# Eight pairs of input-projection tiles a layer as seven block products each, with weight sums by GpSimd

## What is computed

```python
h = _rms_norm(x, mix_norm_g[l])
aq, ak, av, bq, bk, bv, cq, ckv, ckr, gates = _split_cols(h @ w_in[l])   # 512 x6, 384, 256, 32, 3072 columns
oa = differential_attention(aq, ak, av);  ob = dilated_attention(bq, bk, bv);  oc = latent_attention(cq, ckv, ckr)
br = jnp.einsum('bsnc,ncd->bsnd', jnp.stack([oa, ob, oc], axis=2), w_branch[l])
g = jax.nn.sigmoid(gates.reshape(b, s, N_BRANCHES, d))
x = x + jnp.sum(g * br, axis=2) @ w_out[l]
```

## Time and profile before

| | us |
|---|---|
| median of 3 runs | 1645.34 |
| lowest and highest run | 1643.28, 1646.18 |
| span of the profiled execution | 1642.4 |
| PE busy | 1337.7 (81%) |
| DVE busy | 509.3 (31%) |
| ACT busy | 242.0 (15%) |
| POOL busy | 33.6 (2%) |
| mean granted clock of PE | 0.911 |

### The profile page before, as it was taken

How to read it: one execution, slowest core, us unless ns; L and a number is a source line. 1 busy time by engine, 2 the same in 40 slices (tenths; PEclk the granted TensorE clock), 3 DMA queues, 4 the chain that set the end, 5 groups by cost and what they waited for, 6 DMA issues and landing times.

```text
span 1642.4 us, 18217 instructions
## 1 busy us (share of the span) xinstructions
PE 1337.7 (81%) x7594; PEld 793.6 (48%) x7594; DVE 509.3 (31%) x1007; ACT 242.0 (15%) x587; POOL 33.6 (2%) x46
## 2 busy tenths in 40 slices
PE   8999999999666566677699999999996666657655
PEld 7886688755122132233268857886642121312211
DVE  4235464444211211221112462643531211221121
ACT  2214410032010000000021244000410000000002
POOL 2000000001000000000000000000100000000000
PEclk9999999999887888788899999999998787887888
DMA  9933246449999999999995323563699999999996
GB/s 301 328 116 116 78 132 248 175 165 356 412 421 422 420 418 422 421 421 421 419 344 193 122 84 94 192 227 123 250 376 421 421 421 421 419 421 421 421 421 267
DMA packets 143910, 503.87 MB, mean 307 GB/s; under 512 B 9424, under 2 KB 83216, under 8 KB 96720
## 3 DMA queue, kind: packets, MB, share of 16 engines
q1 hardware_dynamic: 140224, 494.41, 77.7%
q0 software_dynamic: 1712, 4.04, 0.8%
q10 hardware_dynamic: 1888, 4.19, 0.7%
HBM read 501.56 MB, written 1.05 MB: 306 GB/s over the span
## 4 chain that ended last, share of the span: by engine, by line
PE 55%; DMA 39%; SPq 2%; DVE 2%; issue 1%; ACT 1%; DVEq 0%; ACTq 0%
DMA ring<-in_w_dram 38%; PE banks L1685 25%; PE banks L1952 6%; PE banks L2020 5%; PE banks L1691 4%; PE banks L2116 3%; SPq L563 2%; PE banks L1849 1%; PE banks L1859 1%; PE banks L1880 1%; PE banks L1901 1%; PE banks L2151 1%; PE banks L2102 1%; PE banks L1743 1%; PE banks L1844 1%
## 5 line engine op out<-in xcount | busy, mean ns | idle before, releaser
L1952 PE MATMUL banks<-ring,v 128*32 128x512 f32 x1888 | 295.8, 759 | 179.4 <-DMA ring<-in_w_dram 168.9
L1685 PE MATMUL banks<-hT,ring 128*128 128x256 f32 x1440 | 317.6, 380 | 0.9 <-ACT kx_wide L836 0.5
L1685 PEld LDWEIGHTS banks<-hT,ring 128*128 128x128 f32 x1440 | 271.9, 190 | 43.3 <-issue 5.3
L1952 PEld LDWEIGHTS banks<-ring,v 128*32 128x32 f32 x1888 | 78.8, 135 | 383.0 <-issue 380.6
L2020 PE MATMUL banks<-ring,probT 128*32 128x512 f32 x960 | 142.6, 716 | 83.6 <-DMA ring<-in_w_dram 76.8
L2020 PEld LDWEIGHTS banks<-ring,probT 128*32 128x32 f32 x960 | 37.3, 129 | 172.7 <-issue 162.6
L1362 DVE COPY q<-banks 128x512 f32<-128x512 f32 x16 | 11.1, 692 | 240.2 <-PE banks L2020 209.2
L1901 PE MATMUL banks<-v,h 128*128 128x128 f32 x512 | 67.0, 293 | 12.1 <-issue 11.7
L1901 PEld LDWEIGHTS banks<-v,h 128*128 128x128 f32 x512 | 63.6, 206 | 26.4 <-issue 26.4
L1358 DVE TENSOR_TENSOR q<-banks,q 128x512 f32<-128x512 f32 x16 | 11.1, 692 | 208.7 <-PE banks L1952 208.7
L1351 DVE TENSOR_SCALAR q<-q 128x512 f32<-128x512 f32 x16 | 6.8, 427 | 162.7 <-ACT q L848 162.7
(11 more groups left out here) (318 smaller groups left out, 1305.3 us busy)
## 6 DMA issues: line engine op xcount, KB each, us to landing
ring<-in_w_dram SPq DMA_DIRECT2D x348, 1024.0 KB, 19.3
ring<-in_w_in_dram SPq DMA_DIRECT2D x52, 1024.0 KB, 9.9
ring<-in_w_branch_dram SPq DMA_DIRECT2D x8, 1024.0 KB, 5.1
ring<-in_w_out_dram SPq DMA_DIRECT2D x8, 1024.0 KB, 5.9
ring<-in_w_dram SPq DMA_DIRECT2D x16, 512.0 KB, 14.4
shared<-in_w_dram SPq DMA_DIRECT2D x6, 1024.0 KB, 5.5
ring<-in_w_branch_dram SPq DMA_DIRECT2D x8, 512.0 KB, 3.4
k<-in_w_dram SPq DMA_DIRECT2D x4, 1024.0 KB, 8.5
```

Source lines behind the costliest of these rows:

```text
L1685: last = nc.tensor.matmul(dst, w[:, k, cols], src[:, k, :], start=k == 0, stop=k == kn - 1)
L1952: last = nc.tensor.matmul(bank[2 + m][e * CAP:(e + 1) * CAP, :], xt[:, k, e * CAP:(e + 1) * CAP], ws[e](r), start=k == 0, stop=k == KD - 1)
```

## The change

Eight pairs of `w_in` tiles a layer are no longer computed as two jobs but as one **double** (`double`): aq, ak, bq, bk (doubles 0 to 3), and gates 4 and 5, 6 and 7, 8 and 9, 10 and 11 (doubles 4 to 7). The product of activations (2 token blocks by 2 K halves) with weights (2 K halves by 2 tiles) is formed from seven block products in place of eight (Winograd's variant of Strassen's scheme).

- **PE**: a block product is 8 matmuls 128x128 by 128x128; a double is 56 of them, in place of 32 with 256 columns. Doubles 0 to 3 now all stand at the start of the layer, before av0; the units of branch A have a job only at every second unit. The gate stage is doubles and branch products in a new order with fixed banks.
- **POOL**: `sum_double` makes the four weight sums of a double, each one tensor_tensor of 128x1024 in SBUF, into two ring slots that SP does not load. Doubles 0 and 1 are summed first in each layer, then the small loads, then doubles 2 to 5, then the router loads and the gain, then doubles 6 and 7.
- **DVE**: `make_halves` forms four sums of blocks of hT (128x512 each) twice a layer; the first time right behind the copies of hT. `join_double` has five instructions of 128x256 for each double. In layer 0 the joins stand behind `set_up_tables`.
- **ACT**: `copy_double` copies five of the block products out of PSUM; for gates `exp_double` follows.
- A layer has 58 turns before the experts in place of 42, and 2 empty turns at its end in place of 6. One preload of an expert tile moves behind the gate doubles. The landing semaphores of a path for overfull experts are halved in number.

The diff, cut to its core:

```diff
+for _at in (OFF_AQ, OFF_AK, OFF_BQ, OFF_BK):
+    add_double(_at, _at + 256)
...
+GATE_DOUBLES = [(4, 5), (6, 7), (8, 9), (10, 11)]
...
+            def sum_double(l, n):
+                at = DOUBLES[n]
+                low, high = (slot_k(at + side, 8, 256) for side in (SIDE_A, SIDE_B))
+                sums = [slot_k(at + SUM_LOW + i // 2, 8, 256)[:, 4 * (i % 2):4 * (i % 2) + 4, :] for i in range(4)]
+                done = (l * ND + n) * 4
+                wait_turn(pool, l, at + SIDE_A)
+                wait_turn(pool, l, at + SIDE_B)
+                pool.wait_ge(slot_free, l * PER_LAYER + (at + SUM_LOW + 1))
+                nc.gpsimd.tensor_tensor(sums[0], low[:, 0:4, :], high[:, 0:4, :], ALU.add).then_inc(sums_made, 1)
+                pool.wait_ge(sums_made, done + 1)
+                nc.gpsimd.tensor_tensor(sums[1], sums[0], high[:, 4:8, :], ALU.add).then_inc(sums_made, 1)
+                pool.wait_ge(slot_free, l * PER_LAYER + (at + SUM_HIGH + 1))
+                nc.gpsimd.tensor_tensor(sums[2], high[:, 0:4, :], high[:, 4:8, :], ALU.add).then_inc(sums_made, 1)
+                pool.wait_ge(sums_made, done + 2)
+                nc.gpsimd.tensor_tensor(sums[3], sums[1], low[:, 4:8, :], ALU.add).then_inc(sums_made, 1)
...
             for l in range(DEPTH):
                 row = one(l)
+                sum_double(l, 0)
+                sum_double(l, 1)
...
+            def make_halves(l, to, late):
...
+                nc.vector.tensor_tensor(to[:, 0], a21, a22, ALU.subtract).then_inc(halves_made, 1)
...
+            def join_double(l, n):
...
+                dve.wait_ge(double_copied, copies + 3)
+                nc.vector.tensor_tensor(high[:, :, 0:P], high[:, :, 0:P], low[:, :, P:], ALU.subtract)\
+                  .then_inc(double_joined, 1)
+                dve.wait_ge(double_made, (l * ND + n) * DOUBLE_MADE + 4)
+                dve.wait_ge(double_joined, done + 1)
+                nc.vector.scalar_tensor_tensor(high[:, :, 0:P], double_bank(n, 2), s, high[:, :, 0:P], ALU.mult, ALU.add)\
+                  .then_inc(double_joined, 1)
...
             for l in range(DEPTH):
                 row = bass.ds(l, 1)
                 copy_hT(l)
+                dve.wait_ge(hT_act, l * COPIES + 2)
+                dve.wait_ge(hT_dve, l * COPIES_DVE + 2)
+                make_halves(l, early_halves, 0)
                 if l == 0:
                     mem_values(0)
                     set_up_tables()
-                for name in ("aq1", "ak1"):
-                    job(l, name)
+                for n in range(NE):
+                    join_double(l, n)
...
+                def others_done(i):
+                    if n % NE >= 2:
+                        if i == 0:
+                            pe.wait_ge(double_copied, (done - 1) * DOUBLE_COPIED)
+                        else:
+                            pe.wait_ge(double_joined, (done - 2) * DOUBLE_JOINED + (5 if i == 1 else 2))
...
+                product(to[0], low[:, 0:4, :], a11, True, ...).then_inc(double_made, 1)
+                others_done(2)
+                pe.wait_ge(halves_made, halves_at + 1)
+                pe.wait_ge(sums_made, done * 4 + 1)
+                product(to[2], sums1[:, 0:4, :], halves[:, 0], True).then_inc(double_made, 1)
...
+                double(l, NE)
+                branches(0)
+                double(l, NE + 1)
+                branches(1)
+                double(l, NE + 2)
+                double(l, NE + 3)
+                branches(2)
+                branches(3)
```

More of the change, by code:

```diff
@@ L121, in add_gate @@
[L121 to L136, removed]
+T_GATE, T_BRANCH = {}, {}
@@ new lines, in gate_col, with add_double, add_branches @@
+def gate_col(g):
+    return OFF_GATE + GATES[g][1] * D + GATES[g][0] * 256
+def add_double(low, high):
+    DOUBLES.append(len(TURNS))
+    TURNS.extend([("in", low), ("in", high), ("sums", 0), ("sums", 1)])
+def add_branches(pair):
+    for n in range(N_BRANCHES):
+        T_BRANCH[pair, n] = len(TURNS) + n // 2
+    TURNS.extend([("branch01", pair), ("branch2", pair)])
+for _at in (OFF_AQ, OFF_AK, OFF_BQ, OFF_BK):
+    add_double(_at, _at + 256)
+T_AV = len(TURNS)
+TURNS += [("in", OFF_AV), ("in", OFF_AV + 256), ("in", OFF_CQ), ("in", OFF_CQ + 256), ("in_last", 3584)]
@@ new lines @@
+T_BV = len(TURNS)
+TURNS += [("in", OFF_BV), ("in", OFF_BV + 256), ("uq", 0), ("uq", 384), ("ukv", 0)]
+T_UQ = T_BV + 2
+for _g in range(EARLY):
+    T_GATE[_g] = len(TURNS)
+    TURNS.append(("in", gate_col(_g)))
+GATE_DOUBLES = [(4, 5), (6, 7), (8, 9), (10, 11)]
+for _pair in range(2):
+    add_double(*[gate_col(_g) for _g in GATE_DOUBLES[_pair]])
+    add_branches(_pair)
+for _pair in range(2, 4):
+    add_double(*[gate_col(_g) for _g in GATE_DOUBLES[_pair]])
+for _pair in range(2, 4):
+    add_branches(_pair)
@@ L357, in bass_hybrid_encoder @@
         main_r, more_r = round_sems("main"), round_sems("more")
[L358 removed]
+        more_landed = [sem(f"more_landed{i}") for i in range(QUAD)]
         more_free = sem("more_free")
@@ L363, in real_turns @@
             return sum(len(CUT_COLS) if CUT <= j < CUT + QUAD else 1 for j in range(upto) if j % RING == slot and
-                       j < PER_LAYER - EMPTY)
+                       j < PER_LAYER - EMPTY and not (j < T_OUT and TURNS[j][0] == "sums"))
         def wait_turn(eng, l, j):
@@ L686, in _ @@
                     load_mcol(l + 1)
+                for n in range(2, NE + 2):
+                    sum_double(l, n)
+                pool.wait_ge(double_joined, (l * ND + NE) * DOUBLE_JOINED)
                 pool.wait_ge(ca_normed, l * 6 + 6)
@@ L702, in _ @@
                 load_gain(ffn_norm_g[row, :])
+                for n in range(NE + 2, ND):
+                    sum_double(l, n)
                 pool.wait_ge(gain_in, l * 16 + 32)
@@ new lines, in _ @@
+                for g in range(3):
+                    sigmoid(g)
+                join_double(l, NE)
+                sigmoid(3)
+                for n in range(3):
+                    mix(0, n)
+                sigmoid(4)
+                sigmoid(5)
+                join_double(l, NE + 1)
+                mix(1, 0)
+                sigmoid(6)
+                mix(1, 1)
+                mix(1, 2)
+                sigmoid(7)
+                join_double(l, NE + 2)
+                sigmoid(8)
@@ L1472, in add_projected @@
+                sigmoid(9)
+                join_double(l, NE + 3)
+                mix(2, 0)
+                sigmoid(10)
+                mix(2, 1)
+                sigmoid(11)
+                mix(2, 2)
+                for n in range(3):
+                    mix(3, n)
                 def add_projected(n, o):
@@ L2058, in _ @@
                 pe.wait_ge(kx_copied, l + 1)
+                for n in range(NE):
+                    double(l, n)
                 job(l, JOB_NAMES[0])
-                pe.wait_ge(vx_copied, l + 1)
-                for name in JOB_NAMES[1:5]:
-                    job(l, name)
                 if l == 0:
```

329 lines of the change are left out of this document (237 added, 92 removed), and 2 rows, old and new, of the table JOBS.

## The result

The changed kernel takes 1676.0 us, median of 4 runs (1672.3 to 1677.2); the kernel before took 1645.8 beside it. The ratio is 1.018, with a 95% interval from 1.0166 to 1.0195: slower, as forecast (1680). The profiled execution has a span of 1670.5 us at a granted clock of 0.902, against 1642.4 and 0.911 before; DVE is busy for 635.3 us and POOL for 189.8, against 509.3 and 33.6.

The account below looks back on a forecast made before the run. PE was taken to bound the mixing part, loads the experts. Layer 0 at +23.0 and layer 1 at +11.4 gave +34.4 on a span of 1642.4: 1676.8, with 2.9 outside it 1680 us; range 1630 to 1695, 8 in 10.

Parts of the forecast that it names:

- Block products: On PE, 0.112 us an instruction, 12.5 us a double against 13.8 for two jobs: 5.3 saved for four doubles.
- POOL's sums: On POOL, a 128x1024 sum takes 2.4 us, four a double 9.6, less than PE's 12.5.
- The late first sums, +2.0: At the very start, turn 1 lands at 27.3 and the first sums come late for PE: 2.0 us added once.
- The tables of layer 0: Layer 0's start: table instructions on DVE take turns with POOL, ending at 78.2; PE waits 23.6 us, plus 2.4 for clock.
- The start of layer 1, +11.1: Seven DVE instructions of the root each wait for a sum: first product 14.0 later, 2.4 for clock, less 5.3.
- Attention, +4.2 a layer: Two sums of double 4 delay DVE at the key rope, +3.2, and double 5's sums add 1.0.
- The 1.0 for double 5: In each layer's attention, double 5's sums fall beside the units of branch C: +1.0 us.
- Gates, -3.9 a layer: Gate stage: 5.9 us saved a layer, less 2.0 of added PE wait.
- The 2.0 that I had added for DVE's lateness: Gate stage: some eight short DVE instructions wait 1 to 2 us each; 2.0 us of PE wait a layer.
- Experts: The experts' part keeps its length, starting earlier or later by whatever the mixing part does.
- Rival A: DVE is hardly held up, by short turns or POOL waiting instead: 1625 us, range 1618 to 1634, chance 20%.
- Rival B: Turns, but cheaper, at 1.28 us a sum: 1645 us, range 1640 to 1662, chance 16%.

Follow-up runs that it names:

- Without sums: The changed kernel with each of GpSimd's 64 additions cut to one element a partition and products reading the low slot instead: 1625.4 us, ratio to before 0.9886.
- with halves: The changed kernel with each sum of 128x1024 made as two additions of 128x512, nothing else changed: 1654.3 us.
- the run with the joins first: The changed kernel with layer 0's joins of doubles 0 and 1 ahead of the table instructions on DVE: 1678.5 us.
- eight additions and eight held instructions: The kernel before, plus eight unread 128x1024 additions on GpSimd at the time of layer 0's tables: 1657.0 us, ratio 1.0069.

## Why the prediction was right, point by point

**Block products.** Forecast 0.112 us an instruction, 12.5 a double. The chain has 25.01 us for 224 instructions in a steady run of the gate stage, 0.112 each; behind the long wait it was 25.79 for 208, 0.124. The short matmul's worse price, with which the Trainium skill (TensorE: Matmul & The Clock Gate, Back-to-back issue gap) speaks against the change, doesn't show in float32: 0.112 us an instruction with 128 columns against 0.216 with 256.

**POOL's sums.** Forecast 2.4; the four groups of 16 have means of 2.43 to 2.50 us.

**The late first sums, +2.0.** Wrong. The first sum began at 24.30, not 27.3: the three loads of which turn 1 is one landed in a median of 12.9 us, not 16.0. What came in the place of this term was one that I had overlooked. I had held DVE's chain from the tables on, but not `make_halves` before it: four instructions of 2.6 to 2.8 us, behind them vx, and PE's third product waiting 5.69 us for vx.

**The tables of layer 0.** Mechanism right, sizes off. Forecast: each held instruction takes one sum, the tables end at 78.2, PE waits from 55.5, 23.6 us. Measured: twelve sums lay beside the tables, and each held one table instruction; it wasn't fourteen, since the sums had begun 3 us earlier and were further on. The four load issues, counted as one instruction each, let three pass: the fifth table instruction took 0.42 us, the sixth 2.32 and the seventh 0.63. The tables end at 71.6, and PE arrived at 61.5, 6 later, for the wait before. The wait was 11.1. Front 0 came to +16.4 instead of +22.7: -5.3, two waits of 5.7 and 11.1, and behind them 1.8 (7.33 for 48, not 5.52) and 2.4 of lower clock make 15.7.

**The start of layer 1, +11.1.** Measured +11.1: 7.6 in the root's column less 2.1 that the last expert load came later, and 5.6 in the front. But its parts don't hold. The first product came 10.9 us later than before relative to the last load, not 14.0: six instructions were held and not seven (L1269 at 861.17 slipped between two sums), and the first sum only began as the root did, at 849.45. The front behind it, forecast at -2.9, came to +0.2: PE waited 1.71, 0.73 and 0.74 us in the first double, ahead of the products that read the second, third and fourth half, and these ended just then (873.00, 875.75 and 878.51); the second had taken 4.06 us, held over two load issues and a sum. Two errors of about 3 us cancelled, which is luck.

**Attention, +4.2 a layer.** Measured +5.4 and +2.6. A sum of double 4 fell on the fold (L1590, 2.82 us against 0.68), and PE waited 3.49 for 0.74. So one sum was in the way and not two, for 2.75 us and not 3.2. In layer 0 another 2.8 is lower clock behind the wait (granted 0.50 from 153.5 to 157.0); in layer 1 the same wait of 3.49 us had a granted clock of 1.00 behind it. The 1.0 for double 5 isn't seen.

**Gates, -3.9 a layer.** Measured -5.8 twice; PE has no wait in there (91.67 busy of 91.67 us). The 2.0 that I had added for DVE's lateness did not come in the change, but came in four other runs to within 0.1, so the term was real, though it was absent where it was forecast.

**Experts.** Forecast 0, measured +2.1 up to the last expert load of layer 0, and +2.2 in layer 1. Without sums it is +1.4 and +1.3, and over all runs these two stretches spread by 2 to 4 us. In layer 1 of the change PE has two waits of 5.67 and 4.92 us, put down to issue, at the gather of the experts, where before had one of 5.88, and the loads fall to 376 GB/s in a slice. The run without sums has two such waits as well, 10.6 us together, so they don't come from the sums. What lengthens the experts wasn't tried and stays open.

The sum of the measured differences is 28.1 of span; the forecast had 34.4. The missing 6 us are those of layer 0's front. Behind it the gates came out 3.8 us below the forecast in all and the experts 4.3 above, and these cancelled by luck: the mechanism was right, and the total is nearer than its terms. Rival A, that DVE is hardly held up, had 1625 us: this is what the kernel takes without the hold (1625.4), though A counted 2.0 for late sums and nothing for the experts, which lost 2.7. Rival B had the price of a turn of 1.28 us at 1645; with halves, whose turn is 1.35 but of which there are twice as many, it was 1654.

**What the pages say.** The hold itself is told by the Trainium skill (SBUF — State Buffer, "SBUF: two separate sides"): an exclusive lock on a pair of ports. The traces here agree: instructions with an operand in PSUM pass (in the run with the joins first L1405 took 0.42 us beside a sum of 2.54), the reciprocals of 128x512 keep their 3.35, and two-input instructions and TENSOR_SCALARs of 128x256 and 128x512 end with the addition. TENSOR_SCALARs of 128x1 passed (0.15 us at 856.56, beside a sum). That the two engines then alternate strictly is what eight additions and eight held instructions show. It is a rule for a chain of such instructions beside sums: one of them slipped through at 861.17, between two sums, and beside load issues it doesn't hold (0.42 and 2.32 us for neighbours at 45 us).

## What to carry to other kernels

Work moved to an idle GpSimd isn't free beside a DVE with short instructions: count the DVE instructions beside it that have two SBUF inputs or are TENSOR_SCALARs from SBUF to SBUF of 256 columns or more, price each at one GpSimd instruction, and look who waits at the end of that queue. Cut GpSimd's instructions to where the hold hurts no more (here 128x512, which cost it 7% more time than whole sums, where 128x256 cost 22%), and let it start behind DVE's chain, not beside it. When a late step is moved back in one queue, look in every other queue for what waits for it: here ACT stood at the sines.

## What I hadn't expected of the hardware

- The turns are exact beside additions: 8 additions of 128x1024 held 8 instructions, 2.31 to 2.52 us each; with 128x512 a held table instruction takes 1.24 to 1.38, with 128x256 0.70 to 0.83.
- Being held works both ways: GpSimd's sum takes 2.35 us alone and up to 2.80 when DVE's instruction of 128x512 is let through before it.
- A wait of PE can cost more than itself: after 11.1 us the next 64 instructions took 9.71 us instead of 7.31, after 8.60 us 32 took 8.84 instead of 7.07. It needn't: after one and the same wait of 3.49 us layer 0 lost another 2.8 at a granted clock of 0.50, and layer 1 nothing at 1.00.
